# Products of zeros given up around the normalisations and ahead of the first dense product

## The chip, the cores and the metric

The kernel runs on one core of a Trainium2 chip, as one program. The metric is the device time of one execution in microseconds (us); of the kernel before it is 1399.15 us, the median of three runs (1398.98, 1399.15 and 1400.94).

## The reference

Two decoder layers over 256 tokens of width 1024, in float32. Layer 0 has a mixer of a causal convolution (31 taps) and a sparse attention, layer 1 a gated short convolution. After the mixer both layers do the same:

```python
x = layer_norm(DN_ALPHA * x + mix, ln_mix_g[layer], ln_mix_b[layer])
x = layer_norm(DN_ALPHA * x + memory_cross_attention(x, mem_k, mem_v, ...), ...)
x = layer_norm(DN_ALPHA * x + hierarchical_moe(x, moe_wg[layer], ...), ...)
# hierarchical_moe: g* = argmax of 4 group logits; top 2 of the 8 experts in it;
# y = sum over the two of gate * (silu(xb @ w1[e]) * (xb @ w3[e])) @ w2[e]
```

There are 32 experts a layer, each with three matrices of 2 MB, so each layer streams 192 MB of expert weights. The three normalisations of each layer are numbered i = 0 to 5 in the kernel (i = 3L for the mixer's, 3L + 1 for the cross-attention's, 3L + 2 for the experts').

## The kernel before

The program is written per engine, without a scheduler: each engine runs its own instructions in the order written, and engines meet at semaphores. SyncE (SP) issues all large weight loads, in the order of their use, each when the buffer that it overwrites is released. The 256 tokens are two tiles t = 0 and 1 of 128; `x` holds them with tokens in partitions, and `xT` holds them turned, in 8 blocks k of 128 features.

**Banks.** TensorE takes the 8 banks of its result memory in rotation (`claim`, L304); a claim waits until the bank's last content has been read out.

**Normalisation.** VectorE adds the residual, takes the statistics and computes the plain normalised row tile (L1176, or ScalarE and VectorE together at L1249 and L1219 behind the experts). TensorE turns the tile (`turned`, L526, products at L538) into two banks. ScalarE (L1262) and VectorE (L1134) write four blocks each into `xT`, with gain and bias, and the next products on TensorE wait block by block (`fresh_part`, L548).

**Products of zeros.** `keep_warm` (L511) issues n products of a 128x128 tile of zeros with a 128x512 operand of zeros, in bfloat16, into a bank that the next real product overwrites. It is called in five places:

- 4 products ahead of the first dense product of the program (L613), after the wait for `xT` and ahead of the wait for the first weights (`av_first`);
- 7 products ahead of the turning of tile 1 of the cross-attention's normalisation (called at L951, issued in `turned`), in both layers. They stand behind `logits(0)`, the router's product of tile 0 (L947), whose result has 36 columns;
- 6 products ahead of the router's product of tile 1 (called at L952, issued in `logits`), in both layers;
- 14 and 4 products ahead of the turning of tiles 0 and 1 behind the experts of layer 0 (L1110 and L1111); the first dense product of layer 1 follows (`by_tile`, L576, and then L568);
- 18 products ahead of the last expert's first product in each layer (L1095). These stay.

**The lead to the experts.** Behind `logits(1)` VectorE multiplies the tile by the gain (L1119), and only then reads the router's result (L1495 and what follows), in the order written. TensorE then claims banks 0 to 3 for the sums of the experts and opens them with four products of zeros of its own (L962, which do a job and stay), adds the residual (L958), counts places (L970 to L976), gathers (L990), and begins the first expert (L1006). Here the claim of bank 1 waits for the router's result of tile 1 to be read out.

**Experts.** Weights lie in 12 buffers, four experts ahead. SP issues an expert's next load when the products that use the buffer are done (L477, waits on `hid_done` and `y_done` of TensorE).

Of the kernel before, what the change touches and what calls it, by code (L numbers as in the profile page):

```python
# [89 lines left out]
def program(nc, T, out):  # L90
    ctx = ExitStack()
    with ctx:
        def sb(name, shape, dt=F32):
            return ctx.enter_context(nc.sbuf_tensor(name, shape, dt))
# [24 lines left out]
        x = sb("x", [P, TT, D])  # L119
# [180 lines left out]
        def wait_loaded(eng, key):  # L300
            s, n = slot_of[key]
            eng.wait_ge(loaded[s], 16 * n)

        def claim(pe, key, bank=None):  # L304

            b = rotation[0] if bank is None else bank
            if bank is None:
                rotation[0] = (b + 1) % 8
            if fills[b]:
                pe.wait_ge(bank_drained[b], fills[b])  # L310
            fills[b] += 1
            bank_of[key] = (b, fills[b])
            return banks[b]

        def filled(ins, key):
            ins.then_inc(bank_filled[bank_of[key][0]], 1)
# [184 lines left out]
        def _(pe):  # L501
# [9 lines left out]
            def keep_warm(ps, n):  # L511

                for _ in range(n):
                    mm(ps[:, :], zero16[:, :], zeros, start=True, stop=True)

            def normal(i, t):

                if i % 3 == 2:
                    pe.wait_ge(act_plain[t], sum((Q, Q // 2)[t] for j in range(2, i + 1, 3)))  # L520
                    if t == 1:
                        pe.wait_ge(dve_plain, Q // 2 * (i // 3 + 1))
                else:
                    pe.wait_ge(n_ready, 2 * (2 * (i // 3) + i % 3) + t + 1)

            def turned(key, src, t, warm=0):  # L526

                for h in range(2):
                    ps = claim(pe, (key, t, h))
                    if h == 0:  # L530
                        keep_warm(ps, warm)
                        if key[0] == "n":
                            normal(key[1], t)
                    if key[0] == "x":
                        pe.wait_ge(x_loaded[t], 16)
                    for k in range(4):
                        cols_ = src[:, t, :].rearrange("p (q k) -> p k q", k=KC)[:, 4 * h + k, :]
                        ins = nc.tensor.transpose(ps[:, k * P:(k + 1) * P], cols_, ident[:, :])  # L538
                    filled(ins, (key, t, h))
# [8 lines left out]
            def fresh_part(i, k, t):  # L548

                c, h = k % 4, k // 4  # L550
                if c < 3:
                    pe.wait_ge((xT_by_act, xT_by_dve)[h], 3 * (TT * i + t) + c + 1)
                else:
                    wait_drained(pe, (("n", i), t, h))
# [6 lines left out]
            def by_weight(fresh, wkey, c0, rhs, ps, last):  # L561

                w = slot(wkey)[:, 0:KC * last].rearrange("p (k n) -> p k n", k=KC)
                for k in AS_TURNED:
                    if fresh is not None:
                        for t in range(TT):
                            fresh_part(fresh, k, t)
                    ins = mm(ps, w[:, k, c0:c0 + P], rhs[:, k, :], start=(k == 4), stop=(k == 3))  # L568
                return ins
# [40 lines left out]
            for c in range(CC):  # L610
                ps = claim(pe, ("a", c))
                if c == 0:
                    keep_warm(ps, 4)  # L613
                    pe.wait_ge(av_first, 16)
                if c == 2:
                    wait_loaded(pe, "av")
                by_weight(None, "av", c * P, xT, ps[:, 0:S], 512)
# [6 lines left out]
            ps = claim(pe, ("cols",))  # L624
# [7 lines left out]
            for j in range(2):  # L632
                ps = claim(pe, ("q", j))
# [8 lines left out]
            ps = claim(pe, ("z",))  # L642
# [4 lines left out]
            ps = claim(pe, ("k",))  # L647
# [4 lines left out]
            for t in range(TT):  # L652
                ps = claim(pe, ("v", t))
# [10 lines left out]
            for j in range(4):  # L664
# [3 lines left out]
                ps = claim(pe, ("mk", j))  # L668
# [5 lines left out]
                if j == 2:  # L674

                    pe.wait_ge(consts_ready, 2)
                    ps = claim(pe, ("cmean",))
# [5 lines left out]
            ps = claim(pe, ("cvar",))  # L683
# [7 lines left out]
            ps = claim(pe, ("ch",))  # L691
# [85 lines left out]
            ps = claim(pe, ("chT",))  # L777
# [8 lines left out]
            ps = claim(pe, ("c2",))  # L786
# [16 lines left out]
            for r in range(2):  # L803
                ps = claim(pe, ("sc", r))
# [28 lines left out]
            for L in range(DEPTH):  # L833
                if L == 1:

                    for h in range(2):
# [12 lines left out]
                        for c in range(4):  # L849
                            ps = claim(pe, ("odb", 4 * h + c))  # L850
# [89 lines left out]
                def logits(t, warm=0):  # L940

                    pe.wait_ge(router_loaded, 16 * 2 * DEPTH)
                    ps = claim(pe, ("lg", L, t))
                    keep_warm(ps, warm)
                    for k in AS_TURNED:
                        fresh_part(3 * L + 1, k, t)
                        ins = mm(ps[:, 0:NG + NE], xT[:, k, t * P:(t + 1) * P], wr[:, L, k, :], start=(k == 4), stop=(k == 3))  # L947
                    filled(ins, ("lg", L, t))

                logits(0)  # L950
                turned(("n", 3 * L + 1), x, 1, 7)  # L951
                logits(1, 6)  # L952

                acc = [claim(pe, ("f", 3 * L + 2, q), bank=q) for q in range(Q)]
                def start_sum(q, t):
# [11 lines left out]
                ps = claim(pe, ("pos", L))  # L967
# [139 lines left out]
                pe.wait_ge(fam.y_ready, first + m + 1)  # L1107
                scatter(fam, comb, y, True)
                if L + 1 < DEPTH:
                    turned(("n", 3 * L + 2), x, 0, 14)  # L1110
                    turned(("n", 3 * L + 2), x, 1, 4)  # L1111

        def gain(st, v, i, t):
# [814 lines left out]
```

## Time and profile before

| | |
|---|---|
| time, median of three runs | 1399.15 us |
| the profiled execution's own time | 1398.52 us |
| its span | 1396.6 us |
| TensorE busy (matmuls) | 1154.3 us, 83% of the span |
| VectorE busy | 395.9 us, 28% |
| ScalarE busy | 169.2 us, 12% |
| moved by DMA | 477.43 MB, mean 342 GB/s |
| mean granted TensorE clock | 0.928 |

### The profile page before, as it was taken

The numbers are of one execution on the slowest core, as the hardware profiler recorded it, in microseconds if no ns is written. First come the engines' busy times: TensorE is split into PE (matmuls) and PEld (weight loads), VectorE is DVE, ScalarE is ACT, GpSimd is POOL, SyncE is SP. The second block draws the span as 40 slices with busy tenths as digits, with TensorE's granted clock in tenths as the row PEclk, the third lists the DMA queues.
The fourth block names the chain that finished last, engine by engine and source line by source line (L and its number), as shares of the span: only waits on it lengthen the run. The fifth ranks groups of instructions, "written<-read, shape, count | busy, mean of one in ns | idle before, by whom it ended". The sixth has DMA issues, their size and how long they took to land.

```text
span 1396.6 us, 33113 instructions
## 1 busy us (share of the span) xinstructions
PE 1154.3 (83%) x11894; PEld 733.7 (53%) x11895; DVE 395.9 (28%) x1046; ACT 169.2 (12%) x473; POOL 28.2 (2%) x77
## 2 busy tenths in 40 slices
PE   8999999988898686677799999999897666766756
PEld 7885548554554353334458867655454333433433
DVE  1872533252232121122123223253232111111213
ACT  0112411111111010001011001111111000000001
POOL 3000000000000000000000000000000000000000
PEclk9999999999999898888899999999999898888888
DMA  9856308479999999999998647455999999999996
GB/s 332 260 181 241 121 31 331 181 271 419 427 428 429 428 428 428 428 428 428 428 416 325 240 159 321 180 222 234 388 429 429 428 428 428 428 428 429 428 428 257
DMA packets 69402, 477.43 MB, mean 342 GB/s; under 512 B 8348, under 2 KB 15804, under 8 KB 44524
## 3 DMA queue, kind: packets, MB, share of 16 engines
q1 hardware_dynamic: 67308, 470.27, 82.3%
q0 software_dynamic: 2048, 6.51, 1.3%
q8 instruction: 34, 0.56, 0.2%
q14 instruction: 12, 0.10, 0.0%
HBM read 473.62 MB, written 3.15 MB: 341 GB/s over the span
## 4 chain that ended last, share of the span: by engine, by line
PE 55%; DMA 27%; SPq 8%; issue 4%; DVE 2%; another core or an unknown queue 1%; ACT 1%; ACTq 1%; POOL 0%; DVEq 0%
DMA ring<-in_moe_w_dram 14%; PE bank L568 13%; DMA slot<-in_moe_w_dram 13%; PE bank L1006 11%; PE bank L589 8%; SPq L477 8%; PE bank L1024 4%; PE bank L1032 3%; PE bank L990 2%; PE bank L770 2%; PE bank L576 2%; PE bank L538 1%; PE bank L891 1%; PE bank L1013 1%
## 5 line engine op out<-in xcount | busy, mean ns | idle before, releaser
L1006 PE MATMUL bank<-ring,xT 128*32 128x256 f32 x1920 | 172.0, 441 | 40.1 <-DMA ring<-in_moe_w_dram 40.1
L1006 PE MATMUL bank<-slot,xT 128*32 128x256 f32 x1120 | 168.8, 468 | 2.2 <-issue 2.2
L568 PE MATMUL bank<-xT,ring 128*128 128x256 f32 x720 | 158.6, 382 | 0.7 <-PE bank L568 0.7
L568 PEld LDWEIGHTS bank<-xT,ring 128*128 128x128 f32 x720 | 137.4, 192 | 20.2 <-issue 1.4
L1006 PE MATMUL bank<-held,xT 128*32 128x256 f32 x608 | 92.9, 473 | 58.6 <-DMA slot<-in_moe_w_dram 49.4
L1006 PEld LDWEIGHTS bank<-ring,xT 128*32 128x32 f32 x1920 | 89.9, 126 | 78.2 <-issue 57.9
L1560 DVE SCALAR_TENSOR_TENSOR xT<-xT,bank 64x256 f32<-64x256 f32 x73 | 30.3, 415 | 349.3 <-ACT xT L1803 349.3
L589 PE MATMUL bank<-ring,slot 128*128 128x512 f32 x256 | 111.5, 593 | 4.1 <-ACT slot L1777 2.2
L1006 PE MATMUL bank<-spare,xT 128*32 128x256 f32 x512 | 76.2, 464 | 43.2 <-DMA ring<-in_moe_w_dram 41.2
L1024 PE MATMUL bank<-ring,xT 128*32 128x256 f32 x1824 | 109.1, 379 | 2.3 <-DVE xT L1570 2.0
L1006 PE MATMUL bank<-gains,xT 128*32 128x256 f32 x512 | 75.8, 461 | 38.6 <-DMA slot<-in_moe_w_dram 38.6
L1032 PE MATMUL bank<-xT 32*128 32x256 f32 x1200 | 87.6, 403 | 20.1 <-issue 18.8
L1006 PEld LDWEIGHTS bank<-held,xT 128*32 128x32 f32 x608 | 48.2, 135 | 98.2 <-issue 85.7
L1546 DVE TENSOR_TENSOR xT<-iota,place 128x64 f32 (+1 forms) x73 | 16.4, 225 | 275.9 <-issue 273.4
L1803 ACT ACTIVATE xT<-bank 64x256 f32<-64x256 f32 x73 | 27.5, 377 | 518.6 <-PE bank L1006 496.2
L1032 PEld LDWEIGHTS bank<-xT 32*128 32x128 f32 x1200 | 55.8, 185 | 55.7 <-issue 52.6
L1024 PEld LDWEIGHTS bank<-ring,xT 128*32 128x32 f32 x1824 | 60.6, 110 | 42.1 <-issue 6.9
L589 PEld LDWEIGHTS bank<-ring,slot 128*128 128x128 f32 x256 | 48.0, 190 | 63.1 <-issue 63.1
L990 PE MATMUL bank<-x,xT 128*32 128x256 f32 x1200 | 80.7, 387 | 0.0
L1006 PEld LDWEIGHTS bank<-spare,xT 128*32 128x32 f32 x512 | 41.5, 132 | 73.7 <-issue 63.8
L1006 PEld LDWEIGHTS bank<-slot,xT 128*32 128x32 f32 x1120 | 76.5, 134 | 3.1 <-issue 2.7
L1006 PEld LDWEIGHTS bank<-gains,xT 128*32 128x32 f32 x512 | 39.2, 132 | 70.0 <-issue 58.2
(281 smaller groups left out, 1097.6 us busy)
## 6 DMA issues: line engine op xcount, KB each, us to landing
ring<-in_moe_w_dram SPq DMA_DIRECT2D x94, 2048.0 KB, 47.3
slot<-in_moe_w_dram SPq DMA_DIRECT2D x46, 2048.0 KB, 48.3
held<-in_moe_w_dram SPq DMA_DIRECT2D x16, 2048.0 KB, 39.6
spare<-in_moe_w_dram SPq DMA_DIRECT2D x16, 2048.0 KB, 46.9
gains<-in_moe_w_dram SPq DMA_DIRECT2D x16, 2048.0 KB, 46.8
ring<-in_od_w_in_dram SPq DMA_DIRECT2D x6, 2048.0 KB, 21.9
ring<-in_xa_wq_dram SPq DMA_DIRECT2D x4, 2048.0 KB, 11.4
ring<-in_xa_wo_dram SPq DMA_DIRECT2D x4, 2048.0 KB, 11.5
```

Source lines behind the costliest of these rows:

```text
L477: sp.dma_start(slot_ap(s), expert_weights(PARTS[m_], L, e + SETS)).then_inc(loaded[s], 16)
L568: ins = mm(ps, w[:, k, c0:c0 + P], rhs[:, k, :], start=(k == 4), stop=(k == 3))
L576: ins = mm(ps[:, t * P:(t + 1) * P], w[:, k, c0:c0 + P], xT[:, k, t * P:(t + 1) * P], start=(k == 4), stop=(k == 3))
L589: ins = mm(ps[:, :], oT[:, k, t * P:(t + 1) * P], ws[h][:, k, :], start=(k == 0), stop=(k == KC - 1))
L770: ins = mm(ps[:, :], memT[:, k, t * P:(t + 1) * P], w[:, k, :], start=(k == 0), stop=(k == KC - 1))
L990: ins = mm(bX[qs[q], 0:w], d[:, t, :], x[:, t, q * w:(q + 1) * w], start=(t == 0), stop=(t == TT - 1))
L1006: ins = mm(b1[qs[2 * m + h], 0:S], xg[:, k, :], ws[m][:, k, h, :, :], start=(k == 0), stop=(k == KC - 1))
L1024: ins = mm(bY[qs[q], 0:n], hidT[:, c, :], w[:, c, q * n:(q + 1) * n], start=(c == 0), stop=(c == 3))
L1032: ins = mm(acc[q][:, t * n:(t + 1) * n], cb[qs[q], t * P:(t + 1) * P], yy[qs[q], :], start=False, stop=final and t == TT - 1, skip_group_c ...
L1546: tt(disp, iota[:, at_].unsqueeze(1).to_broadcast([P, TT, CAP]), column(place, e).to_broadcast([P, TT, CAP]), ALU.is_equal).then_inc(fam.d ...
L1560: stt(out=glu, in0=th, scalar=1.0, in1=banks[5][0:P // 2, 0:S], op0=ALU.add, op1=ALU.mult).then_inc(fam.glu_done, 1)
L1803: act(th, banks[5][0:P // 2, 0:S], ACT.Tanh, scale=0.5).then_inc(fam.tanh_done, 1)
```

## The change

All calls of `keep_warm` but the one of L1095 are given up: 4 products at the start, 13 in each layer's lead to the experts, and 18 behind the experts of layer 0, 48 products in all. Nothing is added or moved.

```diff
@@ -610,7 +610,6 @@
                 ps = claim(pe, ("a", c))
                 if c == 0:
-                    keep_warm(ps, 4)
                     pe.wait_ge(av_first, 16)
@@ -948,8 +947,8 @@
                 logits(0)
-                turned(("n", 3 * L + 1), x, 1, 7)
-                logits(1, 6)
+                turned(("n", 3 * L + 1), x, 1)
+                logits(1)
@@ -1107,8 +1106,8 @@
                 if L + 1 < DEPTH:
-                    turned(("n", 3 * L + 2), x, 0, 14)
-                    turned(("n", 3 * L + 2), x, 1, 4)
+                    turned(("n", 3 * L + 2), x, 0)
+                    turned(("n", 3 * L + 2), x, 1)
```

## Rows read from the trace of the kernel before

**Rows 1.** One line's instructions, L515: count, durations min/median/max in ns, first and last start:

```profile
L515 PE MATMUL bank<-zero x84: 379/379/631, 9.3 to 1374.4; 128*128 128x512 bf16 x84
```

**Rows 2.** Windows: stretch, length, TensorE busy (instructions), granted clock, DMA share, GB/s:

```profile
330.00:700.00 370.00, 283.53 (x4133) 0.89 1.01 428
...
971.00:980.00 9.00, 9.00 (x155) 1.00 0.11 46
981.00:1000.00 19.00, 18.05 (x300) 1.00 1.00 421
```

**Rows 3.** Timeline, start: start, length, engine, line, count [idle before]:

```profile
9.33 1.86 PE L515 MATMUL bank<-zero 128*128 128x512 bf16 x4 [0.88 <-DVE xT L1284]
```

**Rows 4.** One line's DMA, L379 (issued at 1.7), time to landing:

```profile
DMA to landing us min/median/max: 7.6/7.6/7.6
```

**Rows 5.** Groups by form, 11.2 to 13.9 and 14.3 to 20: busy us, mean ns:

```profile
L568 PE MATMUL bank<-xT,ring 128*128 128x256 f32 x7 | 3.2, 628 | 0.0
...
L568 PE MATMUL bank<-xT,ring 128*128 128x256 f32 x28 | 6.2, 380 | 0.0
```

**Rows 6.** Timeline of the lead to the experts of layer 0:

```profile
291.04 1.95 PE L947 MATMUL bank<-wr,xT 128*128 128x36 f32 x16 [0.30 <-PE bank L589]
...
292.82 1.68 PE L515 MATMUL bank<-zero 128*128 128x512 bf16 x7
...
293.87 0.81 DVE L1176 TENSOR_SCALAR x<-x,mv,rstd 128x1024 f32<-128x1024 f32 x1
...
294.74 1.16 PE L538 MATMUL bank<-ident,x 128*128 128x128 f32 x8 [0.24 <-DVE x L1176]
...
295.73 1.46 PE L515 MATMUL bank<-zero 128*128 128x512 bf16 x6
296.00 1.36 DVE L1134 TENSOR_SCALAR xT<-bank,lngT 128x128 f32<-128x128 f32 x4 [0.24 <-PE bank L538]
...
297.02 1.87 PE L947 MATMUL bank<-wr,xT 128*128 128x36 f32 x16
...
297.85 1.23 DVE L1119 TENSOR_TENSOR x<-x,gains 128x1024 f32<-128x1024 f32 x1
298.99 0.15 DVE L1495 TENSOR_TENSOR g<-bank,rbias 128x4 f32<-128x4 f32 x1
...
299.47 1.02 PE L962 MATMUL bank<-zero 128*128 128x512 bf16 x4 [0.58 <-issue]
...
300.33 1.89 PE L958 MATMUL bank<-x,residual 128*128 128x256 f32 x8
```

**Rows 7.** Timeline behind the experts of layer 0:

```profile
729.69 3.19 PE L515 MATMUL bank<-zero 128*128 128x512 bf16 x14
734.67 1.16 PE L538 MATMUL bank<-ident,x 128*128 128x128 f32 x8 [1.79 <-ACT x L1249]
...
735.52 0.54 DVE L1219 TENSOR_SCALAR x<-bank,mv,rstd 128x256 f32<-128x256 f32 x1 [0.16 <-DVE x L1219]
...
735.67 1.03 PE L515 MATMUL bank<-zero 128*128 128x512 bf16 x4
...
737.42 3.74 PE L576 MATMUL bank<-xT,ring 128*128 128x128 f32 x32
```

**Rows 8.** Timeline of TensorE ahead of a fall of the clock, and windows:

```profile
138.88 3.32 PE L808 MATMUL bank<-gains,slot 64*128 64x15 f32 x32
142.79 0.67 PE L713 MATMUL bank<-slot 64*128 64x256 f32 x2 [0.60 <-DVE gains L1383]
...
144.00:146.00 2.00, 2.00 (x5) 0.50 0.00 0
```

**Rows 9.** The chain of waits, experts of layer 0: start, length, what:

```profile
442.21 6.29 PE bank L1006 x64
...
500.93 5.35 PE bank L1006 x64
...
510.44 3.50 PE bank L1006 x64
```

## The prediction

> **What bounds the kernel now.** I read the chain of waits first. From the first product to about 320 us it runs mostly through TensorE, and again from the end of the experts of layer 0 to about 980 us. Inside the two expert stages it runs through DMA. The windows say the same: from 330 to 700 us the DMA moves 428 GB/s without a pause, while from 971 to 980 us it moves 46 GB/s and TensorE is busy throughout, and from 981 us it is full again [rows 2]. In layer 1 the loads wait for buffers that TensorE frees until then. So TensorE's time counts up to the point where the DMA fills up (about 311 us in layer 0, 981 us in layer 1). A delay ahead of it moves all loads behind it and so the end; a delay inside the full stretch is hidden. All four places of the change lie where TensorE counts. Next I looked at the products of zeros by their line: 84 in all, 379 ns in the median [rows 1], of which 48 go. Then at the timeline around each place, for what the next product waited for, and last at the windows, for where the clock fell and what TensorE had done before.
>
> **The start, 4 products.** They occupy 9.33 to 11.19 us [rows 3] at the lower level: the products of L568 behind them take 628 ns up to 13.9 us and 380 ns from 14.3 us [rows 5], so the clock rises at about 14. What they waited for, VectorE's copy (L1284), releases them at 9.33 [rows 3]. The first weights, for which the product behind them waits, land at 1.7 + 7.6 = 9.3 us [rows 4], so neither is late. Without them the dense products begin 1.86 us earlier. If the clock rises at the same moment, those 1.86 us are won at the lower level and are worth half, 0.9 us. The ends are 0 (the weights land later, and the zeros filled the wait) and 1.86 (the rise comes earlier as well). I take -0.9; the gain stays, since the chain runs through TensorE from there.
>
> **The leads to the experts, 13 products in each layer.** First without the clock. The 7 products run from 292.82 to 294.50, but the turning behind them waits for L1176, which ends at 294.68 [rows 6]: they are hidden behind VectorE, worth 0. The 6 products end about 297.1 and delay the router's product, which without them could begin at about 296.5, when the first blocks of xT are written (L1134 from 296.00 on), and end near 298.0 in place of 298.9. But what reads it is L1495 on VectorE, and that stands behind L1119 in VectorE's order: L1119 ends at 299.08, and L1495 starts at 298.99, back to back (in this trace a VectorE record starts some 0.09 us before the last one ends) [rows 6]. L962 starts at 299.47, behind L1495 and its neighbour. So VectorE hides these 6 too: 0, with 1.3 us as the far end (the chain of waits does put them on the path).
>
> Now the clock. Without the zeros TensorE has, from 291.0 to 299.5 us, only the two router's products, 36 columns wide, 8 short turnings of 0.9 us, and gaps of 1.7, 0.6 and 1.5 us. The nearest row is at 139 to 144 us: TensorE was counted busy for 3.3 us with products 15 columns wide, stood still for 0.6 us, and the clock is at 0.50 right behind [rows 8]. The stretch of the lead is longer and as thin, so I expect the clock to fall, between 293.5 and 297 us, and to rise only when wide products (L958 from 300.33, L1006 from 306 on) have run for a while, at 303 to 306 us. The price from rows: of a fall in the expert stage, the 64 products of L1006 take 5.35 or 6.29 us in place of 3.50 [rows 9], 1.9 to 2.8 us. In the lead, the turning can double (+0.9), the router's product takes +1.7 of which 0.9 is the slack in front of L1495 (+0.8), L962 doubles (+0.9), and up to 1.3 of L958's 1.7 is added [rows 6]: 3.9 at most, with the earliest fall. A late fall spares the turning and half of the rest: 2.2. No fall: 0. The stretch of layer 1 is the same with the same lengths. I take +3.0 each, +6.0.
>
> What follows a late first expert: the loads that its end releases are the ones the DMA waits for (the DMA is nearly empty then), so it is passed on whole in both layers.
>
> The Trainium skill (TensorE: Matmul & The Clock Gate, "HAM oscillation — how this bites in real kernels") tells of falls from one unbroken idle gap, as between bursts that wait for a DMA. By that rule the leads, whose longest gap becomes 1.7 us, would keep the upper level and cost nothing, and the sum would be +0.3 us; the fall behind L808, with only 0.6 us idle, speaks against it here.
>
> **Behind the experts of layer 0, 18 products.** The 14 run from 729.69 to 732.9; the turning behind them waits for L1249 and starts at 734.67 [rows 7]. Worth 0 in time, but without them TensorE stands still for 4.9 us, and the slowed products of the expert stage stand behind such pauses, in which TensorE waits for a load [rows 9]. So a fall is nearly certain. The 4 products delay the turning of tile 1: they end at 736.7, and what it needs (L1219) ends at 736.06 [rows 7], worth 0.5 us. Behind it come L576 and 38 us of dense products, all on the path. The fall comes between 731.8 and 735.2, the rise between 737.3 and 740.7. At the lower level lie both turnings (0.9 each) and 0 to 2.4 us of L576; the waits for ScalarE's and VectorE's blocks take some of it. Loss 0.9 to 2.6, less the 0.5: +0.4 to +2.1. I take +1.2. The ends are -0.5 (no fall) and +2.8, the dearer of the falls in rows 9.
>
> **Sum.** -0.9 + 2 x 3.0 + 1.2 = +6.3 us. The profiled execution took 1398.52 us (span 1396.6), so 1404.8; the median is 0.6 higher, 1399.15, and gives 1405.4.
>
> **The rivals.**
> A. The clock stays up in the leads, and falls only behind the experts. For it: no gap there is longer than 1.7 us. Against: rows 8. Time: -0.9 + 0 + 1.2 = +0.3, 1399.5.
> B. The products were simply on the path, and the clock does not fall. The chain has 1.86 us of them at the start, 1.3 in each lead, and 0.9 behind the experts. It would take L1495 not being tied to L1119, and the clock holding through 4.9 us of standing still. Time: -1.9 - 2.6 - 0.5 = -5.0, 1394.2; with half of it, 1396.7. It decides where VectorE is ready before TensorE at 299 us. Against: rows 6 show a tie, and long gaps do lower the clock.
> C. The falls come, but DMA that is queued ahead hides them in the leads: the first experts' weights were loaded beforehand, and the stage ends by DMA. It needs loads queued past the first expert's end. Against: 46 GB/s at 971 to 980 [rows 2]. Time as in A, 1399.5.
>
> **How the numbers follow.** The forecast has 0.70, A 0.15, C 0.08, B 0.07. The forecast's own range is -0.9 + 2 x (2.2 to 3.9) + (0.4 to 2.1), that is +3.9 to +9.0: 1403.0 to 1408.2. The range reaches down to A and C, to 1399.0, and up to 1409.5, where the start gives nothing and both leads cost all. A difference of 0.2% (2.8 us) is about what a measurement of this kernel can tell from no change. Slower by more has the forecast's 0.70 and 0.02 from A and C with dearer falls: 0.72; within it lie the rest of A and C and a little of B: 0.22; faster: 0.06.
>
> **What would show it.** In the profile after, the clock at 0.50 between about 294 and 305 us and at the same place ahead of the first expert of layer 1, with L958 at 600 ns and more; a first L1006 of layer 0 about 3 us later, less the start's 0.9; the clock at 0.50 from about 734 to 739 us; L568's first product at about 9.4 us. The step on the start is wrong if 0.9 us is not gained by 40 us. Wrong altogether if the windows of the leads show 1.00.

## The result and the profile after

The changed kernel takes 1406.88 us, the median of six runs (1405.78 to 1412.39), against 1399.16 for the kernel before in as many. The ratio is 1.0066 with a 95% interval of 1.0050 to 1.0082: slower by 7.7 us by the medians and by 9.2 us (7.0 to 11.5) by the ratio, where +6.3 was forecast. The ratios here and below leave out single executions far above the others of their kernel (one of e1 at 5654 us, one of e12 at 1668, and two of the kernel before, at 1560 and 1416). The profiled execution of the changed kernel took 1407.34 us, with a span of 1405.5 (before 1396.6) and a mean granted clock of 0.917 (before 0.928).

The timeline of the lead to the experts of layer 0, TensorE alone. Behind the first edit every line number is one lower than before: L946 was L947, L957 was L958, L961 was L962, L1005 was L1006.

```profile
289.69 1.95 PE L946 MATMUL bank<-wr,xT 128*128 128x36 f32 x16 [0.30 <-PE bank L589]
293.48 1.94 PE L538 MATMUL bank<-ident,x 128*128 128x128 f32 x8 [1.84 <-DVE x L1175]
296.09 3.60 PE L946 MATMUL bank<-wr,xT 128*128 128x36 f32 x16 [0.67 <-DVE xT L1133]
300.21 1.86 PE L961 MATMUL bank<-zero 128*128 128x512 bf16 x4 [0.53 <-issue]
301.87 2.34 PE L957 MATMUL bank<-x,residual 128*128 128x256 f32 x8
...
308.27 0.41 PE L1005 MATMUL bank<-held,xT 128*32 128x256 f32 x2
```

The windows over the same stretch (columns as in [rows 2], here with each engine's busy time ahead of the clock: TensorE, its weight loads, VectorE, ScalarE, GpSimd):

```profile
290.00:292.00 2.00, 1.64 (x15) 1.52 (x14) 1.24 (x5) 0.00 (x0) 0.73 (x2) 1.00 0.77 180
292.00:293.00 1.00, 0.00 (x0) 0.00 (x0) 0.93 (x5) 0.00 (x0) 0.06 (x1) 0.76 0.96 393
293.00:294.00 1.00, 0.52 (x3) 0.55 (x4) 0.90 (x5) 0.00 (x0) 0.00 (x0) 0.50 1.07 459
...
302.00:303.00 1.00, 1.00 (x5) 0.79 (x4) 0.96 (x3) 0.00 (x0) 0.00 (x0) 0.62 0.00 0
303.00:304.00 1.00, 1.00 (x6) 0.90 (x5) 0.48 (x1) 0.00 (x0) 0.00 (x0) 1.00 0.06 16
```

The clock fell at about 292.5 us, while TensorE waited for VectorE, and rose at about 302.8. In between TensorE's products took 1.7 to 1.9 times as long: the 8 records of the turning 1.94 us against 1.16, the router's second product 3.60 against 1.87, L961 1.86 against 1.02 [rows 6]. VectorE no longer hides the router's product; it now waits for it:

```profile
299.72 0.16 DVE L1494 TENSOR_TENSOR g<-bank,rbias 128x4 f32<-128x4 f32 x1 [1.13 <-PE bank L946]
```

In layer 1 the clock fell later in the lead, 4.8 us behind its start and not 2.8, and rose later, at about 947.9 us. The turning ran at the upper level there, but L957 ran at the lower one, and this lead was the dearer one:

```profile
936.61 1.13 PE L538 MATMUL bank<-ident,x 128*128 128x128 f32 x8 [1.84 <-DVE x L1175]
938.41 3.60 PE L946 MATMUL bank<-wr,xT 128*128 128x36 f32 x16 [0.67 <-DVE xT L1133]
...
944.19 3.62 PE L957 MATMUL bank<-x,residual 128*128 128x256 f32 x8
```

Behind the experts of layer 0 (timeline, then two windows of TensorE):

```profile
731.90 1.15 PE L1031 MATMUL bank<-xT 32*128 32x256 f32 x16 [0.49 <-ACT xT L1808]
738.06 3.65 PE L538 MATMUL bank<-ident,x 128*128 128x128 f32 x16 [5.01 <-ACT x L1248]
741.50 4.49 PE L576 MATMUL bank<-xT,ring 128*128 128x128 f32 x32
745.83 38.15 PE L568 MATMUL bank<-xT,ring 128*128 128x256 f32 x176
```

```profile
736.00:737.00 1.00, 0.00 (x0) 0.63 1.07 393
...
743.00:744.00 1.00, 1.00 (x10) 0.96 1.04 383
```

TensorE stands still for 5.0 us, the clock falls in that pause and is back only at 743.1; both turnings (3.65 us for what took 2.2) and part of L576 (4.49 against 3.74 in [rows 7]) run at the lower level.

The start, one row (compare [rows 3]; in the trace before, the dense products of L568 begin at 10.99 us):

```profile
9.54 29.39 PE L568 MATMUL bank<-xT,ring 128*128 128x256 f32 x128 [1.08 <-DMA ring<-in_ev_w_in_dram]
```

A bill of the two profiled executions, from the timelines' start times:

| stretch | before | after | difference |
|---|---|---|---|
| start of the span to the first router's product of layer 0 | 291.04 | 289.69 | -1.35 |
| from there to the first expert's first product | 15.25 | 18.58 | +3.33 |
| experts of layer 0, to the end of the last scatter | 423.47 | 424.78 | +1.31 |
| from there to the end of L576 | 11.40 | 12.94 | +1.54 |
| to the first router's product of layer 1 | 186.83 | 186.83 | 0.00 |
| from there to the first expert's first product | 15.25 | 19.15 | +3.90 |
| experts of layer 1 and the last normalisation | 453.36 | 453.53 | +0.17 |
| span | 1396.6 | 1405.5 | +8.9 |

The term that belongs to no edit is the +1.31 in the experts of layer 0. That stretch took between 424.8 and 427.6 us in the profiled executions of the experiments below, and it differs between kernels that have the same program in it (424.9 in e1 and e5, 427.5 in e3), so it is a spread between executions. Part of what varies is a pause behind the first expert's first products (L1006), in which TensorE waits for nothing that the profile shows: 4.4 us before and 1.1 us after, 4.3 to 4.6 us in e3, e8, e9, e11 and e12, 1.0 to 2.6 us in the others. It alone does not order the lengths of the stretch, and its cause is open.

### The profile page after: what moved, and what is told of

It reads as the page before. It is cut to its first block, busy times and chain, and to the rows that moved or that the text cites. A ratio compares the mean times of both kernels' runs of the same rounds, so it can differ in the third digit from the quotient of the medians.

```text
span 1405.5 us, 33020 instructions
## 1 busy us (share of the span) xinstructions
PE 1155.1 (82%) x11846; PEld 736.1 (52%) x11847; DVE 396.4 (28%) x1046; ACT 169.6 (12%) x473; POOL 28.2 (2%) x77
## 4 chain that ended last, share of the span: by engine, by line
PE 54%; DMA 30%; SPq 8%; issue 4%; DVE 2%; ACT 1%; ACTq 0%; DVEq 0%; POOL 0%
DMA ring<-in_moe_w_dram 17%; PE bank L568 13%; DMA slot<-in_moe_w_dram 13%; PE bank L1005 11%; PE bank L589 8%; SPq L477 7%; PE bank L1023 4%; PE bank L1031 2%; PE bank L989 2%; PE bank L769 2%; PE bank L576 2%; PE bank L890 1%; PE bank L538 1%; PE bank L946 1%; PE bank L908 1%
## 5 line engine op out<-in xcount | busy, mean ns | idle before, releaser
L1005 PE MATMUL bank<-ring,xT 128*32 128x256 f32 x1920 | 172.8, 444 | 41.2 <-DMA ring<-in_moe_w_dram 41.2
L1005 PE MATMUL bank<-slot,xT 128*32 128x256 f32 x1120 | 168.9, 468 | 2.8 <-issue 2.8
L568 PE MATMUL bank<-xT,ring 128*128 128x256 f32 x720 | 158.7, 382 | 1.8 <-DMA ring<-in_ev_w_in_dram 1.1
L568 PEld LDWEIGHTS bank<-xT,ring 128*128 128x128 f32 x720 | 137.2, 192 | 21.2 <-issue 2.5
L1005 PE MATMUL bank<-held,xT 128*32 128x256 f32 x608 | 92.8, 473 | 57.3 <-DMA slot<-in_moe_w_dram 48.4
L1005 PEld LDWEIGHTS bank<-ring,xT 128*32 128x32 f32 x1920 | 90.1, 127 | 80.4 <-issue 60.2
L1005 PE MATMUL bank<-spare,xT 128*32 128x256 f32 x512 | 75.6, 461 | 42.5 <-DMA ring<-in_moe_w_dram 41.9
L1005 PE MATMUL bank<-gains,xT 128*32 128x256 f32 x512 | 76.1, 462 | 37.0 <-DMA slot<-in_moe_w_dram 37.0
L1005 PEld LDWEIGHTS bank<-held,xT 128*32 128x32 f32 x608 | 48.1, 135 | 96.9 <-issue 84.3
L1005 PEld LDWEIGHTS bank<-slot,xT 128*32 128x32 f32 x1120 | 76.7, 134 | 4.5 <-issue 4.5
L1005 PEld LDWEIGHTS bank<-spare,xT 128*32 128x32 f32 x512 | 40.1, 132 | 73.8 <-issue 62.8
L1005 PEld LDWEIGHTS bank<-gains,xT 128*32 128x32 f32 x512 | 39.4, 132 | 67.2 <-issue 55.0
## 6 DMA issues: line engine op xcount, KB each, us to landing
ring<-in_xa_wq_dram SPq DMA_DIRECT2D x4, 2048.0 KB, 11.5
```

The source lines that it names most:

```text
L1005: ins = mm(b1[qs[2 * m + h], 0:S], xg[:, k, :], ws[m][:, k, h, :, :], start=(k == 0), stop=(k == KC - 1))
```

## Experiments

Two stretches are measured in every trace: the **lead**, from the start of the first router's product to the first expert's first product (15.25 us before, in both layers), and the **turn**, from the end of the last scatter of layer 0 to the end of L576 (11.40 us before). Ratios are to the kernel before in the same session, with 95% intervals; 0.001 is 1.4 us, and differences in us are taken from the ratios. Each kernel was traced in one execution; moments of the clock are read from it.

**e1, the start alone.**

```diff
-                    keep_warm(ps, 4)
```

> Only the 4 products ahead of the first dense product are given up. Theory (the clock rises at the same moment, and the products stood on the path at the lower level): 0.9 to 1.4 us faster than the kernel before, the first L568 at about 9.5 us, the first router's product of layer 0 (L946 or L947) at about 289.7 us in place of 291.0, and the clock at 1.00 from 285 to 310 us. Rival (the products held the clock up or filled the wait for the weights): no gain, and dense products at 628 ns beyond 14 us.

Ratio 0.9988 (0.9977 to 0.9999), 1.7 us faster, with 0.1 to 3.2 in the interval. In its trace the clock rose at about 8 us already, and the products began at 9.68 us, held by the weights. The theory's direction holds, but not its premise that the rise stays put: over the traces of e1 to e10, before and after it came between about 7.2 and 15.7 us (it shows in the length of the products, as in [rows 5]), with the 4 and without them, and that moves the end of the first dense block by more than the 4 products do. So traces have to be compared at like rises:

| rise at about | end of the first dense block with the 4 | without the 4 |
|---|---|---|
| 7.2 to 8.1 | 37.45 (e3), 37.86 (e4) | 37.54 (e1) |
| 12.5 to 12.7 | 39.48 (e8), 39.60 (e9) | 38.93 (after) |
| 14.0 and 15.7 | 40.28 (before, 14.0) | 40.49 (e6, 15.7) |

At a rise near 12.6 the 4 products are worth 0.6 us; at an early rise they cost next to nothing, as the first weights hold the dense products to about 9.5 us. The times bear the gain out only weakly: e1's interval just misses no change, and e6, which also gives up the 4, is no faster than e8, which keeps them (see below).

**e2, both leads alone** (`turned(("n", 3 * L + 1), x, 1)` and `logits(1)`, all else as before).

> Only the 13 products in each layer's lead to the experts are given up. Theory (they held the clock up): slower by 4.5 to 8 us, with the clock at 0.50 for 6 to 10 us in each lead, and the router's second product at 3.6 us in place of 1.9. Rival (they only cost time on the path, as the chain of waits has it): faster by up to 2.6 us, no fall in the leads. A third (the DMA queued ahead hides it): falls, but less than 1.5 us slower in all.

Ratio 1.0063 (1.0045 to 1.0081), 8.8 us slower. The leads took 20.17 and 18.62 us, +4.9 and +3.4, with the clock at 0.50 for 13.7 and 10.2 us. The theory holds in its mechanism, but the time and the length of the falls both lie above what it gave (8 us, and 10 us of the lower level). The rival "on the path" falls by its sign, and the third one because the leads' 8.3 us appear in the time.

**e3, behind the experts of layer 0 alone** (14 and 4 given up).

> Only the 18 products behind the experts of layer 0 are given up. Theory: slower by 0.4 to 2.1 us; TensorE stands still for 5 us, the clock is at 0.50 for 3 to 7 us around the turnings, L576 begins up to 1 us later relative to the last product of the experts than in the kernel before, and L568 up to 2 us later. Rival (no fall): 0.5 us faster.

Ratio 1.0008 (0.9999 to 1.0017), +1.1 us, with no change just inside the interval. The trace shows the cause: the turn took 13.02 us, +1.6, with the clock at 0.50 from about 734.2 to 741.1 us. The three parts e1, e2 and e3 add up to 8.2 us, against 9.2 for the whole change by its ratio; the difference is within the intervals.

**e4, only the 7 given up,** and **e5, only the 6.**

```diff
e4: -                turned(("n", 3 * L + 1), x, 1, 7)
    +                turned(("n", 3 * L + 1), x, 1)
e5: -                logits(1, 6)
    +                logits(1)
```

> Only the 7 products ahead of the turning of tile 1 are given up in both leads; the 6 stay. Theory (all 13 together hold the clock, and the 7 lie in VectorE's shadow): the clock falls in some or all leads since TensorE's widest gap is back, but for a shorter while: slower by 1 to 6 us. If the 6 suffice: no difference, since the 7 were hidden. If the 7 were on the path: faster by up to 1.5 us.

> Only the 6 products ahead of the router's second product are given up in both leads; the 7 stay. The chain of waits has these 6 on the path, 1.3 us a layer. If the clock holds, this tells whether they were: theory (VectorE's L1119 stands before L1495 anyway): the first L1006 begins at the same moment behind the first router's product as before, within 0.1 us, and the time is the same. Rival B: 1.0 to 1.3 us earlier in each layer, 2 to 2.6 us faster. If the clock falls: slower by 2 to 6 us.

e4: ratio 1.0067 (1.0052 to 1.0081), 9.4 us slower. e5: 1.0001 (0.9991 to 1.0012), no difference. The timelines of the lead of layer 0, first e4:

```profile
288.46 1.95 PE L947 MATMUL bank<-wr,xT 128*128 128x36 f32 x16 [0.30 <-PE bank L589]
292.24 1.94 PE L538 MATMUL bank<-ident,x 128*128 128x128 f32 x8 [1.83 <-DVE x L1176]
293.98 2.76 PE L515 MATMUL bank<-zero 128*128 128x512 bf16 x6
296.54 3.46 PE L947 MATMUL bank<-wr,xT 128*128 128x36 f32 x16
300.53 1.87 PE L962 MATMUL bank<-zero 128*128 128x512 bf16 x4 [0.53 <-issue]
```

and e5, with two of VectorE's rows:

```profile
292.28 1.68 PE L515 MATMUL bank<-zero 128*128 128x512 bf16 x7
...
296.02 1.95 PE L947 MATMUL bank<-wr,xT 128*128 128x36 f32 x16 [0.67 <-DVE xT L1134]
...
297.31 1.23 DVE L1119 TENSOR_TENSOR x<-x,gains 128x1024 f32<-128x1024 f32 x1
298.46 0.15 DVE L1495 TENSOR_TENSOR g<-bank,rbias 128x4 f32<-128x4 f32 x1
...
298.94 1.02 PE L962 MATMUL bank<-zero 128*128 128x512 bf16 x4 [0.97 <-issue]
```

In e5 the router's second product starts 5.52 us into the lead in place of 5.98 and ends 0.4 us sooner, and all of that is given back in front of L962 (0.97 us idle against 0.58 in [rows 6]). L1495 stands back to back behind L1119, the lead is 15.25 and 15.24 us, and the clock stays at 1.00. So the 6 neither cost nor hold anything. In e4 the 7 are missing, the clock falls, and the 6 now lie on the path at the lower level, 2.76 us of them: the leads take 21.12 and 20.95 us, with 13.7 us at the lower level in each. In e2, without all 13, the lead with a fall of the same length took 20.17 us, 0.8 to 0.9 us less. The times of e4 and e2 don't tell the two apart. e4's expectation had the fall but missed its size: it gave a shorter fall and at most 6 us.

**e7 and e10, narrow products in the gaps.** The 7 and 6 products become products of the same zeros with 16 columns, 24 and 20 of them in e7, 56 and 46 in e10.

```diff
+                    if n < 0:
+                        mm(ps[:, 0:16], zero16[:, :], zero16[:, 0:16], start=True, stop=True)
```

> The leads' 7 and 6 products of zeros, 512 columns wide, become 24 and 20 products 16 columns wide, which fill about the same time. Theory (the clock fell behind L808 because TensorE did only narrow products before, so that filling the gaps with narrow ones does not hold it): the clock falls in both leads as it does with nothing in the gaps, and the time is 4.5 to 8 us above the kernel before. Rival (only an unbroken gap lowers the clock, so anything in it helps): 1.00 throughout the leads, and no difference in time.

> As e7, but with 56 and 46 narrow products in each lead, since 24 filled only 0.75 us: the gaps of TensorE are then filled (1.4 us each at the upper level), and no gap is longer than in the kernel before. Theory (narrow products do not hold the clock): it falls in both leads, 5 to 12 us slower. Rival (only an unbroken gap lowers the clock): 1.00 throughout the leads, the kernel before's time.

e7: ratio 1.0081 (1.0066 to 1.0096), 11.3 us slower. Its 24 products filled only 0.75 us, leaving a gap of 1.17 us, so e7 alone does not decide. Its leads took 18.58 and 18.48 us, 6.6 us in all; its trace loses 5.5 us more in the last stretch (experts of layer 1 and last normalisation, 458.9 us against 453.4), where the pause behind the first expert's first products is 4.3 us (0.7 to 1.7 in layer 1 of all other traces) and the clock falls once more, at 959.3 us. Why this pause is long in some executions is open, so e7's time is not the price of its leads alone. e10: 1.0081 (1.0059 to 1.0102), 11.3 us slower. Its timeline, and windows of TensorE:

```profile
290.33 1.95 PE L950 MATMUL bank<-wr,xT 128*128 128x36 f32 x16 [0.30 <-PE bank L592]
292.11 1.59 PE L516 MATMUL bank<-zero 128*128 128x16 bf16 x56
294.02 1.97 PE L541 MATMUL bank<-ident,x 128*128 128x128 f32 x8 [0.33 <-DVE x L1179]
295.79 1.42 PE L516 MATMUL bank<-zero 128*128 128x16 bf16 x46
297.06 3.61 PE L950 MATMUL bank<-wr,xT 128*128 128x36 f32 x16
```

```profile
290.00:294.00 4.00, 3.39 (x73) 0.89 0.74 250
...
293.00:294.00 1.00, 0.69 (x27) 0.54 0.91 377
...
294.00:296.00 2.00, 1.98 (x15) 0.50 0.94 393
```

TensorE is counted busy for 85% of 290 to 294 us (3.39 of 4.00) and pauses for no longer than 0.33 us, and the clock falls at about 293.1 all the same; the leads take 20.40 and 20.51 us. Seven products of 512 columns in the same gap hold it (e5, without the 6). The narrow products did not even delay the fall: it came 2.6 to 3.0 us behind the start of the lead in all leads of e2, e4, e7 and e10, and 2.8 and 4.8 us behind it in the changed kernel. In the 9 traces that keep the 7 wide products the clock holds in both leads, in the 5 without them it falls in both. The rule of the unbroken gap, rival A, is refuted for this place.

**e6, e8, e9: which of the 18 hold the clock.** e8 gives up the 4 alone, e9 the 14 alone, e6 the 4 and the start's 4.

> Given up: the 4 products at the start, and the 4 between the two turnings behind the experts of layer 0. Their 14 and the leads' 13 stay. Theory: the start gives 0.9 to 1.4 us, the 4 give 0.5 us with the clock held by the 14: faster by 1.4 to 1.9 us in all. Rival (the 4 are needed to hold the clock behind the 14): a fall at about 736 us, and no gain.

> Only the 4 products between the two turnings behind the experts of layer 0 are given up; the 14 stay. First theory (the prediction's): 0.5 us faster, as the 4 delayed the second turning. Theory after e6: the 14 alone do not hold the clock through the wait for ScalarE and the turnings; it falls near the second turning in most executions, and from the last scatter of layer 0 to the end of L576 it takes about 12.8 us in place of 11.4: 0.5 to 1.5 us slower.

> Only the 14 products behind the last scatter of layer 0 are given up; the 4 stay. Theory: TensorE stands still for 4.9 us, the clock falls before the first turning, and the 4 then run at the lower level on the path, 1.7 us in place of 0.9: 1.5 to 3 us slower, more than without any of the 18 (1.1 us in e3). Rival (the 4 bring the clock back sooner): no more than in e3.

Ratios: e6 1.0005 (0.9996 to 1.0015), e8 1.0004 (0.9994 to 1.0015), e9 1.0017 (1.0006 to 1.0027). The turn took 12.77, 12.77 and 13.93 us. The timeline of e8, and two windows:

```profile
732.79 3.20 PE L515 MATMUL bank<-zero 128*128 128x512 bf16 x14
737.77 1.17 PE L538 MATMUL bank<-ident,x 128*128 128x128 f32 x8 [1.78 <-ACT x L1249]
739.30 1.81 PE L538 MATMUL bank<-ident,x 128*128 128x128 f32 x8 [0.37 <-DVE x L1219]
740.90 4.73 PE L576 MATMUL bank<-xT,ring 128*128 128x128 f32 x32
```

```profile
738.00:740.00 2.00, 1.63 (x12) 0.89 1.05 387
740.00:742.00 2.00, 2.00 (x12) 0.50 1.05 388
```

Without the 4 the second turning does come 0.3 us sooner behind the first, but the clock falls at about 739.6 and the turn is 1.4 us longer, in e6 (739.3) as in e8. In the 9 traces that keep all 18 it does not fall there, so 14 and 4 are needed together. The times don't tell e8 or e6 from no change: e8's runs spread from 1396.2 to 1403.6 us and the profiled one is the slowest, so how often the clock falls there is open. e9 is the dearest of the three by its trace, though its interval overlaps the others: the 4 then run on the path at the lower level, 1.91 us. The rival, that they bring the clock back sooner, falls: in e9 as in e3 the clock is at 0.50 from 3.4 to 10.2 us behind the last scatter. e6's expectation of 1.4 to 1.9 us faster was a miss.

**e11 and e12, eight products while TensorE waits for x.**

```diff
             pe.wait_ge(zero_ready, 1)
+            keep_warm(banks[7], 8)
```

> The 4 products at the start are given up, and 8 are issued ahead of the very first turning, while TensorE waits for x (0.9 to 4.8 us); all else as before. Theory: the clock's rise, at 7 to 16 us in the executions so far, comes at 4 to 9 us; the dense products of the start gain half of what they ran at the lower level: 2 to 3.5 us faster than the kernel before, and faster than e1. Rival (the rise does not depend on what runs before x arrives): as e1, 1 to 2 us faster, with rises up to 16 us.

> As e11, but the 4 products ahead of the first dense product stay. Theory: with the clock at the upper level by then the 4 cost 0.9 us on the path, less what they hide of the wait for the first weights (0.3 to 1.0 us in the executions without them): 0 to 0.6 us slower than e11, still 1.5 to 3 us faster than the kernel before. If the rise in e11 is sometimes late because TensorE pauses ahead of the first dense product, this one is as fast as e11 or faster.

e11 (the 4 given up): 1.0002 (0.9990 to 1.0013). e12 (the 4 kept): 0.9986 (0.9978 to 0.9995), 2 us faster, the best kernel of the study together with e1, whose interval overlaps it. The first rows of e11, then of e12, each with L568 by form between 9.5 and 11 us:

```profile
4.42 2.76 PE L538 MATMUL bank<-ident,x 128*128 128x128 f32 x16
...
9.67 29.50 PE L568 MATMUL bank<-xT,ring 128*128 128x256 f32 x128 [2.48 <-DMA ring<-in_ev_w_in_dram]
...
L568 PE MATMUL bank<-xT,ring 128*128 128x256 f32 x3 | 1.6, 677 | 2.5 <-DMA ring<-in_ev_w_in_dram 2.5
```

```profile
7.69 1.02 PE L515 MATMUL bank<-zero 128*128 128x512 bf16 x4 [0.88 <-DVE xT L1285]
9.55 27.89 PE L568 MATMUL bank<-xT,ring 128*128 128x256 f32 x128 [0.84 <-DMA ring<-in_ev_w_in_dram]
...
L568 PE MATMUL bank<-xT,ring 128*128 128x256 f32 x7 | 1.8, 394 | 0.8 <-DMA ring<-in_ev_w_in_dram 0.8
```

In e11 the early products raised the clock, so that the turnings took 2.76 us in place of 3.65, but TensorE then waited 2.5 us for the first weights with nothing to do, the clock fell again (0.50 from 9.6 to 13.0 us), and the dense products began at the lower level, at 677 ns. The 2 to 3.5 us that e11's theory expected were a miss; the 1 to 2 us of its rival lie at the edge of the interval. In e12 the 4 fill that wait, and the dense products start at 394 ns; their block ends at 37.44 us, as early as in e3, where the clock happened to rise at 7.2 us. The 4 that the change gave up as mere cost become useful, by these traces, once the products ahead of them come early enough (the intervals of e11 and e12 overlap a little).

## Why the prediction was right, by its steps

- **Which stretch counts.** Right. The two leads' delays were not taken up by the DMA: e2's leads grow by 8.3 us and its time by 8.8 (6.3 to 11.3), e10's by 10.4 and 11.3, so rival C (hidden by queued loads) is refuted. The experts' stretches do not get shorter behind late leads either (424.78 against 423.47 us, and 453.53 against 453.36).
- **The start, -0.9.** Right in sign as far as e1 shows (-0.1 to -3.2 us). The trace's -1.35 is partly luck: the rise moved from about 14.0 to 12.6 us between the two traces, and at like rises the 4 products are worth 0.6 us. Two steps fail: "the clock rises at the same moment" (7.2 to 15.7 us over all traces), and that the dense products begin 1.86 us earlier. They began 1.45 us earlier, at 9.54, as the first weights now held them (1.08 us idle <-DMA); half of 1.45 is the 0.7 that the working would then have given.
- **The leads without the clock, 0.** Right, and shown by e5 for the 6: the chain of waits listed them with 1.3 us a layer, and giving them up changes nothing, since VectorE's order sets L1495.
- **The leads' clock, +3.0 each.** The mechanism was right; the size was somewhat low: +3.33 and +3.90 in the profile after, +4.9 and +3.4 in e2. Counted from the start of the lead (291.04 before, 289.69 after), the falls were forecast 2.5 to 6.0 us in and came 2.8 and 4.8 us in. The pricing by the moment of the fall failed: a late fall was to be the cheap one (2.2, which is also not what "spares the turning and half of the rest" gives; 3.9 less 0.9, halved, is 1.5). Layer 1's late fall did spare the turning, and cost more, since the lower level lasted as long (10.2 us in both leads) and so reached through L957. What sets the price is how long the lower level lasts and what lies in it: with 10.2 us a lead costs 3.2 to 3.9 us, with 13.7 us (e2's first lead, both of e4 and e10) 4.9 to 5.9, above the 3.9 that was given as the most.
- **Behind the experts, +1.2.** Right: +1.54 in the trace, +1.1 in e3; the lower level lay 3.2 to 10.0 us behind the last scatter, where 2.0 to 5.4 was forecast for the fall and 7.5 to 10.9 for the rise. One part of it failed: the 4 products "worth 0.5 us". They also help to hold the clock: in e8 and e6, which give them up and keep the 14, it fell, and the turn was 1.4 us longer.
- **The sum, +6.3.** The medians say +7.7 and the ratio +9.2 (7.0 to 11.5). The terms that belong to the edits give +7.4 in the trace: the gain at the start came out larger than forecast by the chance of the rise, and the leads 1.2 us dearer.
- **Rival A** (no fall in the leads, by the rule of the unbroken gap): refuted by every trace without the 7, most sharply by e10. **Rival B** (products simply on the path): refuted by e2 and e5; only at the start are the products on the path, and there for 0.6 us and not 1.9.

## What to carry over

A filler product on an idle engine is judged twice: by what it delays, and by what the clock does without it. The chain of waits shows only the first, and even that wrongly where another engine is ready at the same moment. Here fillers paid where a wait of 1.8 to 5 us stood ahead of TensorE work that sets the end, with only narrow or short products around it. Give them up one place at a time: 7 of the 13 in a lead held its clock, and the other 6 did nothing, except that they lay on the path once the 7 were gone.

## What the runs showed of the hardware

- The granted clock fell with TensorE counted busy 85% of the time and no pause above 0.33 us, when what it did was products of 16 and 36 columns (e10); with 7 products of 512 columns in the place of the narrow ones it held. Here the busy share of the profile did not tell whether the clock holds.
- The first rise of the clock came between about 7.2 and 15.7 us after the start of the span in the traces of before, after and e1 to e10, and the end of the first dense block moved with it from 37.5 to 40.5 us. That may be part of why the runs of the kernel before spread over 6 us in a session (1396.4 to 1402.3); the experts of layer 0, whose stretch varies by 4 us between traces, may be another part, and no run separates them.
- The ten falls in the leads lasted 10.2 or 13.7 us each, and cost 3.2 to 5.9 us of a lead of 15.25 us.
